# A two-layer backbone step: modulation by channel halves, and table work and scan steps in other places

## What is computed

```
for l in range(2):
    for s in (context, latent):            # with c_ctx and with c
        shift, scale, gate = split(silu(cond[s]) @ w_ada[l] + b_ada[l], 3)
        h = rmsnorm(x[s], norm_g[l]) * (1 + scale) + shift
        z = h @ w_in[l]                    # ca, cg | ssm, sg | q, kv, ag | 3 x 1024 merge
        ya = silu(layernorm(depthwise_conv31(ca * sigmoid(cg))))
        br_a = (ya * silu(conv_gate)) @ w_conv_out[l]
        y  = d * ssm + scan forwards + scan backwards   # complex diagonal state space
        br_b = (glu(gelu(y) @ w_ssm_glu[l]) * silu(sg)) @ w_ssm_out[l]
        q, k = rmsnorm per head (latent: rotary too); latent also reads context keys and values
        br_c = (attention(q, k, v) * silu(ag)) @ w_attn_out[l]
        mixed = sigmoid(m_a) * br_a + sigmoid(m_b) * br_b + sigmoid(m_c) * br_c
        x[s] += gate * (mixed @ w_out[l])
outputs: x of both streams, keys and values of the context, its final scan states
```

## Time and profile before

| | |
|---|---|
| median of 3 runs | 786.66 us (784.63 to 787.0) |
| profiled execution | 783.96 us, its span 782.2 us, mean granted TensorE clock 0.937 |
| TensorE, its weight load | busy 667.8 us (85%), 477.0 us (61%) |
| VectorE, ScalarE, POOL | 567.1 us (73%), 298.8 us (38%), 36.2 us (5%) |
| transfers | 117.65 MB, 46.7% of 16 engines on SP's queue |
| chain that ended last | PE 36%, DVE 13%, ACT 2%, issue 2%, of the span |

### The profile page before, as it was taken

How to read it: one execution, slowest core, us unless ns; L and a number is a source line. 1 busy time by engine, 2 the same in 40 slices (tenths; PEclk the granted TensorE clock), 3 DMA queues, 4 the chain that set the end, 5 groups by cost and what they waited for, 6 DMA issues and landing times.

```text
span 782.2 us, 9620 instructions
## 1 busy us (share of the span) xinstructions
PE 667.8 (85%) x3578; PEld 477.0 (61%) x3578; DVE 567.1 (73%) x1063; ACT 298.8 (38%) x452; POOL 36.2 (5%) x50
## 2 busy tenths in 40 slices
PE   4539999999778799775989499999978679999997
PEld 1337774446644588664768387555556348877875
DVE  3776486794885899889765634948878688998564
ACT  1354351113544244351543534311345334444442
POOL 2010200210000000010000200011000000000000
PEclk9978999999897999986999799999999789999999
DMA  8754267841453556521445145583051025665531
GB/s 252 290 200 134 72 231 252 281 158 33 184 193 113 147 184 181 168 81 32 158 135 160 54 135 197 173 299 109 18 199 28 27 81 162 189 188 161 189 116 54
DMA packets 63209, 117.65 MB, mean 150 GB/s; under 512 B 11052, under 2 KB 15484, under 8 KB 63164
## 3 DMA queue, kind: packets, MB, share of 16 engines
q1 hardware_dynamic: 62988, 116.98, 46.7%
q10 hardware_dynamic: 176, 0.07, 0.0%
HBM read 112.51 MB, written 1.38 MB: 146 GB/s over the span
## 4 chain that ended last, share of the span: by engine, by line
PE 36%; DVE 13%; ACT 2%; issue 2%; POOL 1%; POOLq 0%; DVEq 0%; ACTq 0%
PE proj L1050 8%; PE proj L1052 8%; PE proj L1051 8%; PE proj L767 7%; DVE qkt L1372 3%; DVE H L1372 2%; PE side L782 1%; PE side L990 1%; PE side L899 1%; DVE cvacc L1444 1%; DVE pre L1372 1%; PE side L1068 1%; DVE raw_split L1372 1%; POOL st L1853 1%; DVE mixed L1372 1%
## 5 line engine op out<-in xcount | busy, mean ns | idle before, releaser
L767 PE MATMUL proj<-raw,hT 128*128 128x512 f32 (+1 forms) x320 | 132.0, 558 | 0.0
L1444 DVE SCALAR_TENSOR_TENSOR cvacc<-cvpad,taps,cvacc 128x256 f32<-128x256 f32 x240 | 98.3, 478 | 0.2
L767 PEld LDWEIGHTS proj<-raw,hT 128*128 128x128 f32 x320 | 58.2, 190 | 59.4 <-issue 57.8
L1051 PE MATMUL proj<-raw_split,H_split 128*128 128x512 f32 x224 | 90.1, 402 | 0.0
L1108 ACT ACTIVATE wide_split<-raw 128x1024 fp32r<-128x1024 f32 x59 | 61.9, 1058 | 72.6 <-PE proj L1052 72.6
L1372 DVE TENSOR_TENSOR raw_split<-raw,wide_split 128x1024 fp32r<-128x1024 f32 x59 | 71.4, 1220 | 19.0 <-ACT wide_split L1108 18.5
L1050 PE MATMUL proj<-wide_split,H_split 128*128 128x512 f32 x140 | 58.4, 417 | 15.2 <-DVE raw_split L1372 14.8
L1052 PE MATMUL proj<-wide_split,H_split 128*128 128x512 f32 x140 | 56.5, 403 | 0.0
L1051 PEld LDWEIGHTS proj<-raw_split,H_split 128*128 128x128 f32 x224 | 44.1, 197 | 9.3
L1108 ACT ACTIVATE utok_split<-raw 128x1024 fp32r<-128x1024 f32 x29 | 30.7, 1057 | 37.1 <-PE proj L1052 37.1
L1372 DVE TENSOR_TENSOR raw_split<-raw,utok_split 128x1024 fp32r<-128x1024 f32 x29 | 35.4, 1221 | 10.7 <-ACT utok_split L1108 10.3
(11 more groups left out here) (236 smaller groups left out, 1314.5 us busy)
## 6 DMA issues: line engine op xcount, KB each, us to landing
raw<-in_w_in SPq DMA_DIRECT2D x104, 512.0 KB, 3.7
raw<-in_w_ada SPq DMA_DIRECT2D x48, 512.0 KB, 5.3
raw<-in_w_out SPq DMA_DIRECT2D x16, 512.0 KB, 3.8
raw<-in_w_ssm_glu SPq DMA_DIRECT2D x8, 512.0 KB, 6.8
raw<-in_w_ssm_out SPq DMA_DIRECT2D x8, 512.0 KB, 3.7
raw<-in_w_attn_out SPq DMA_DIRECT2D x8, 512.0 KB, 3.7
raw<-in_w_conv_out SPq DMA_DIRECT2D x8, 512.0 KB, 3.8
raw<-in_w_in SPq DMA_DIRECT2D x8, 256.0 KB, 3.7
```

The costliest lines, as they stand in the source:

```text
L767: m = T.matmul(proj.bank((l, u, s))[:, 0:n], lhs[:, s, kt, :], w[:, i, :], start=(kt == 0), stop=last)
L1051: T.matmul(bank[:, :], hi, wlo, start=False, stop=False)
L1444: m = V.scalar_tensor_tensor(acc, src, taps[:, t, j:j + 1], acc, ALU.mult, ALU.add)
```

## The change

- A modulation slab now holds shift and scale of half the channels (two runs of 512 columns) instead of one of the two for all. `hT` and `early` go by channel half instead of by stream, ScalarE modulates stream 0 and VectorE stream 1. Units cg and ssm run in halves (`HALVED`): two slabs of cg and two of ssm on the first channel half, then the rest.
- In the prologue the loads of x and of the modulation rows stand before those of the table c. The first channel half is normed, split and half of pre made before the rest of the modulation arrives.
- `preP` is taken apart into `bbar` and `pre(l, half)`. In layer 1 too, the second half of pre now stands in unit cg/ssm and its `preE` behind `pack`, ahead of POOL's `bz`. For layer 1's tables, `tabA` moves ahead of C0, `tabB` ahead of C1's `cback`, `bT` and `bbar` behind A0, the first half of pre behind A1 and its `preE` behind the output projection; their loads are issued in comb B0 instead of B1.
- All 32 scan steps stand before attention, six of them ahead of unit q. QK norm squares and sums both streams first, then scales. Twelve convolution taps follow the scan, the first attention has four in each of five parts, the second six, and B0, B1 and C0 have 14, 14 and 10.
- The end of the first attention (a reciprocal and two products) and the gate gg are done within `Y`.

```diff
-    return ([("hT", 0), ("hT", 1), ("early", 0), ("early", 1), ("chunks", "cg"), ("unit", "cg")]
-            + ([("preP", 0, 1)] if l == 0 else [])
-            + [("unit", "ssm"), ("unit", "ca"), ("pack",)] + ([("preE", 0, 1)] if l == 0 else [])
-            + [("bz", 0), ("UT",), ("S",), ("cp",), ("convT", 0), ("convT", 1), ("unit", "q"), ("unit", "kv"),
-               ("adaE", l, 2), ("qkn", 0), ("qkn", 1), ("scan",), ("unit", "sg"), ("K", 0), ("bz", 1),
+    return (([("hT", 0), ("early", 0)] if l else [])
+            + [("chunks", "cg"), ("hT", 1), ("early", 1), ("half", "cg"), ("half", "ssm"), ("unit", "cg"), ("pre", l, 1),
+             ("unit", "ssm"), ("unit", "ca"), ("pack",), ("preE", l, 1),
+             ("bz", 0), ("UT",), ("S",), ("cp",), ("convT", 0), ("convT", 1), ("scan", 0, 6), ("unit", "q"), ("unit", "kv"),
+             ("adaE", l, 2), ("qkn",), ("scan", 6, NCHUNK), ("conv", 12, None), ("unit", "sg"), ("K", 0), ("bz", 1),
...
-            + [("qkT", 0), ("att", 0), ("unit", "gg"), ("Y",), ("adaT", l, 2)] + nxt("adaT", n, 0)
+            + [("qkT", 0), ("att", 0), ("Y",), ("adaT", l, 2)] + nxt("adaT", n, 0)
...
-            + [("chunks", "meB0"), ("brT", "B", 0), ("brT", "B", 1), ("conv", 20, "B0"), ("comb", "B", 0),
-               ("brT", "C", 0), ("brT", "C", 1), ("conv", 20, "B1"), ("comb", "B", 1)]
-            + nxt("small", n) + nxt("cT", n) + [("conv", 20, "C0"), ("comb", "C", 0)]
-            + nxt("taps", n) + nxt("tabA", n) + [("cback", 0), ("cback", 1), ("comb", "C", 1)]
-            + nxt("tabB", n) + nxt("bT", n) + nxt("preP", n, 0) + [("brT", "A", 0), ("brT", "A", 1), ("comb", "A", 0)]
-            + nxt("preE", n, 0) + nxt("preP", n, 1) + [("comb", "A", 1)] + nxt("preE", n, 1)
-            + [("wout", 0), ("wout", 1)] + nxt("xn", n, 0) + nxt("xn", n, 1))
+            + [("chunks", "meB0"), ("brT", "B", 0), ("brT", "B", 1), ("conv", 14, "B0"), ("comb", "B", 0)]
+            + nxt("small", n) + [("brT", "C", 0), ("brT", "C", 1), ("conv", 14, "B1"), ("comb", "B", 1)]
+            + nxt("cT", n) + nxt("tabA", n) + [("conv", 10, "C0"), ("comb", "C", 0)]
+            + nxt("taps", n) + nxt("tabB", n) + [("cback", 0), ("cback", 1), ("comb", "C", 1)]
+            + [("brT", "A", 0), ("brT", "A", 1), ("comb", "A", 0)]
+            + nxt("bT", n) + nxt("bbar", n) + [("comb", "A", 1)] + nxt("pre", n, 0)
+            + [("wout", 0), ("wout", 1)] + nxt("preE", n, 0) + nxt("xn", n, 0) + nxt("xn", n, 1))
...
-                src = A["w_ada"][key[1]].rearrange("(k p) n -> p k n", p=P)
-                slabs.append((key, 1, D, src[:, key[3]:key[3] + 1, D * key[2]:D * key[2] + D]))
+                src = A["w_ada"][key[1]].rearrange("(k p) (r x) -> p k r x", p=P, x=W)[:, key[3], :, :]
+                slabs.append((key, 2, W, src[:, 4:6, :] if key[2] == 2 else src[:, key[2]:4:2, :]))
...
                 elif k == "qkn":
-                    s = stg[1]
...
+                    needs("h")
+                    for s in range(NS):
+                        proj.drained(dve, (l, "q", s))
+                        proj.drained(dve, (l, "kv", s))
+                        link(tt_(qkt[:, :], qk[:, s, :], qk[:, s, :]))
+                        V.tensor_reduce(qst[:, s, 0, :], qkt[:, :].rearrange("p (h d) -> p h d", d=HD), AX_X,
+                                        ALU.add).then_inc(qk_sq, 1)
+                        dve.wait_ge(qk_sq, ls(l, s))
+                    for s in range(NS):
+                        qk_norm(l, s)
...
-                        if s == 0:
-                            c0 = STEPS_BEFORE_ATT + STEPS_IN_ATT * p
-                            for c in range(c0, c0 + STEPS_IN_ATT):
-                                for i in range(4):
-                                    scan_step(l, c, i)
-                        else:
-                            for _ in range(8):
-                                conv_tap(*taps_left.pop(0))
+                        for _ in range(6 if s else 4):
+                            conv_tap(*taps_left.pop(0))
```

More of the change, by code:

```diff
@@ L126, in units_of @@
 def units_of(stage):
-    if stage[0] == "unit":
+    if stage[0] in ("unit", "half"):
         u = stage[1]
@@ L400, in build @@
         slab_used = sem("slab_used")
[L402 to L403 removed]
+        pieces = [key for key in order_of_slabs if key[0] != "ada" and split_unit(key[1])]
         piece_at = {key: m for m, key in enumerate(pieces)}
@@ L1016, in _ @@
                     m.then_inc(side.full, 1)
-                if k in ("unit", "comb", "wout") and stg[1] not in IN_ATT_UNITS:
+                if k in ("unit", "half", "comb", "wout") and stg[1] not in IN_ATT_UNITS:
                     for u, nk, n in units_of(stg):
@@ L1094, in merged_high, with gate @@
                                  ACT.Copy, scale=0.5).then_inc(split_hi, 1)
+            def gate(l, u):
+                for s in range(NS):
+                    key = (l, u, s)
+                    proj.filled(act, key)
+                    S.activation(gates[:, GATE[u], s, :], proj.bank(key)[:, :], ACT.Silu).then_inc(proj.freed(key), 1)
             highs = [0]
@@ L1615, in _ @@
-                        for i in range(2):
-                            side.drained(dve, ("bT", ll, i))
-                        for r in range(2):
-                            t1, t2 = (parts[j][:, :, r if j == 0 else 1 - r, :].rearrange("p c g -> p g c") for j in range(2))
-                            makes("bbar", tt_(bbar[:, r, :, :], t1, t2, ALU.add if r else ALU.subtract))
                         side.filled(dve, ("cT", ll, 1))
-                        needs("bbar")
                     else:
```

256 lines of the change are left out of this document (140 added, 116 removed).

## The result

| | before | changed |
|---|---|---|
| median of 20 runs each, side by side | 784.57 us (782.79 to 787.22) | 787.05 us (785.53 to 788.55) |
| ratio, 95% interval | | 1.0025 (1.0016 to 1.0035) |
| span of the profiled execution | 782.2 us | 784.7 us |
| mean granted TensorE clock | 0.937 | 0.942 |

The change makes the kernel 2.5 us slower: the side that was forecast, at 0.6 of the 4.2 us. The sum was wrong by 1.7 us, and by much more within, since the errors of its terms partly cancel. The forecast of 790.9 stands 3.9 above the measured 787.05; 2.1 of that is its starting point, 786.66, the median of three runs, where the median of twenty is 784.57.

The account below looks back on a forecast made before the run. TensorE's pace was taken as the bound, with gaps nearly all ended by VectorE instructions. Terms 9.0 + 3.2 - 4.7 - 8.1 + 5.0 - 1.1 + 0.9 = +4.2 on the median 786.66 gave 790.9 us, range 780 to 798.

Parts of the forecast that it names:

- term 1: Start of attention: key copy 7.35 us later; +9.0 in layer 1 with a restart, +3.2 in layer 0 with half a one.
- term 2: Scan's output and second attention: earlier HY copy and fewer taps ahead of the GELU sums, -4.7 us over both layers.
- term 6: Prologue: half the modulation needed, but split and half of pre queue on VectorE; +0.9 us (bounds -2 and +2).
- term 3: Layer 0's combinations and output projection: C0 +5.9, C1 -0.95, A0 -17.9, A1 -0.7, output projection +5.55; together -8.1 us.
- Term 4: Layer 1's first projections: pre's other half between two slab residues, with half a restart and 16 transposes, +5.0 us.
- Term 5: From layer 0 to 1: second stream's normalisation without POOL's work beside it, -1.1 us (bounds -2.5 and +1).
- That row is the nearest, so I take 1.5: QK norm: VectorE holds POOL up, as at 705.60, so the rearranged norm saves 1.5 us; ends 0 and 3.65.
- restart: TensorE's clock at 1.2 GHz after a wait: 1.65 us behind longer waits, half (0.8) behind waits near 2.4 us.
- Within the first attention ... so nothing: First attention: four taps (1.65 us) replace two scan steps (2.1), but VectorE waits for TensorE each step; no gain.
- POOL is not held up: Rival, QK norm: saves 3.65 us instead of 1.5, key copy 5.2 later; 785.8 us, chance 0.22.
- The second: Rival: TensorE keeps 2.4 GHz across the new waits, all restarts (6.55 us) fall out; 784.35 us, chance 0.15.
- The third: Rival: the rearranged QK norm saves nothing because POOL's operations are held, +3.8 us; 794.7 us, chance 0.13.

Follow-up runs that it names:

- x_qkn: Changed kernel with the QK norm done one stream after the other, as before; ratio to the kernel before 1.0083, span 789.0 us.
- x_warm: Changed kernel with the key transpose of layer 1's first attention done 48 times instead of once; ratio to the kernel before 0.9995, span 782.7 us.
- x_taps: Changed kernel with the twelve convolution taps ahead of attention put back into the combinations, both layers; ratio to the kernel before 0.994, span 778.9 us.
- x_attend: Changed kernel with the first attention's end done ahead of the scan's output again; ratio to the kernel before 1.0035, span 783.4 us.
- x_att8: Changed kernel with eight taps instead of six per part of the second attention, ten fewer in the combinations; ratio to the kernel before 1.0059, span 788.0 us.
- x_pre0: Changed kernel with layer 1's first half of pre made in the output projection's second half; ratio to the kernel before 0.9947, span 778.9 us.
- x_best3: x_best2 with both halves of layer 0's pre moved behind first units and cut by residues; median 749.99 us, ratio to the kernel before 0.9557.
- x_best2: Changed kernel with x_pre0's move, x_taps in layer 1 alone, and tabA, tabB and pre's second half cut by residues; median 756.42 us, ratio to the kernel before 0.9646.

## Why the prediction was right or wrong, point by point

**The step that failed.** Measured less forecast, the sum was off by -2.3 us in term 1, -2.2 in term 2 and -0.8 in term 6, and by +2.9 in term 3 and +0.5 in terms 4 and 5 together; that +2.5 came out, on the side of the forecast, is these errors cancelling, and so in good part luck. The step that failed is in term 1: "That row is the nearest, so I take 1.5." The QK norm saved 2.54 us in each layer instead, and x_qkn shows 2.6 and 2.7 of it at the key copies, so the term was 1.0 too dear twice. Three smaller steps failed beside it. A restart had one price, 1.65, by the length of the wait; the runs show from 1.4 to 3.0, and none behind the waits of 1.51 and 2.56 to which half a one was given. Term 2 put the shorter filling at nothing and the taps at 1.2 a layer; 0.8 is left for the one, and the other measured 1.45 to 1.6. Term 3 put B0 at nothing; it lost 1.1.

**What bounds the kernel: right in the main.** The waits that the edits moved end with a VectorE instruction: those that the earlier trace rows names, and beside them H_split (403.21) and, in the prologue, pre (53.32). The edits that took VectorE's work from ahead of them gave the time back. Not all long waits are VectorE's, though: in the second attention four of 2.6 to 3.3 us end with ScalarE in the trace of before, and the change hardly moved them.

**Term 1, attention's start: right in layer 1 by two errors, wrong in layer 0.** Layer 1 measured +6.0 for the key copy and +2.9 for the restart (x_warm), 8.9 for a forecast of 9.0. The QK norm saved 2.54 and not 1.5, the twelve taps cost 4.6 and not 4.9 (x_taps), the restart cost 2.9 and not 1.65. The step "That row is the nearest, so I take 1.5" failed: POOL was held up once, by 0.6, and the second time by 0.4, not until the first stream was scaled. The Trainium skill ("SBUF — State Buffer", "Who interferes with whom") has a VectorE instruction with two SBUF inputs contend with a POOL instruction that reads SBUF. The trace agrees in kind, as the 0.84 at 517.27 shows; the size is the measured one, 0.6 and 0.4, and VectorE's own products beside POOL's second root (521.15, two in 1.02) take what they take in x_qkn with POOL idle. In layer 0 the same 6.0, less 4.93, gives 1.0; TensorE then waited 1.51, and "half a restart" did not come. Forecast +3.2, measured +1.0.

**Term 2, scan's output and second attention: direction right, size short.** Measured -4.6 in layer 0 and, with the restart taken out, -2.3 in layer 1, against -2.9 and -1.8. The step "Within the first attention ... so nothing" failed in part: the filling in its last part counts (0.8), and the move of the attention's end counts 1.6 up to the HY copy, though it comes back behind it (x_attend). The taps fewer are worth 1.45 to 1.6 a layer (x_att8), not 1.2. A restart that the term did not have also plays in: behind the 4.04 us at 203.99 the clock of before was 0.50, behind the 2.08 at 202.83 it was 1.00. The other traces of this order, where it fell there, take 0.3 to 0.6 longer in the stretches behind.

**Term 3, combinations: the mechanism right in each stage, the sum 2.9 too good.** A0 (-18.1 for -17.9), A1 and the output projection (+5.6 for +5.55) came as priced, C1 and C0 0.5 and 1.0 worse. C0's wait was 4.76 for 4.25, and the restart behind it 2.5 for 1.65 (twelve slow matmul spacings, 0.43 against 0.23); in C1 it was 2.2 where before it was 1.4 (eleven for seven). B0 and B1 had no price and lost 1.7: 1.1 of it in B0, whose wait is the same (3.31 for 3.26), but whose clock stayed at 0.50 over the first 5.28 us, while the trace of before has

```profile
264.82:270.10 5.28, 5.28 (x17) 4.26 (x18) 4.90 (x8) 0.86 (x1) 0.00 (x0) 0.73 0.41 121
```

In layer 1, B0 of before had the slow stretch too. In layer 0 all eleven traces of the changed order have it, at 0.50 or 0.51 over the first 5 us; whether the 0.73 of before was its rule or chance stays open, since there is one trace of it.

**Term 4, layer 1's units:** +5.4 for +5.0, by two errors. The wait of 2.56 and the transposes of 1.9 are as priced; the half restart behind the wait did not come here (it did in x_pre0), but the one at the first matmul of cg, which had no price, took 2.8 where before it took 1.9. **Term 5:** -1.0 for -1.1. **Term 6:** the first matmul came 1.8 later, not 0.9, and the units took 1.7 less, so +0.1 up to Uz. The 1.7 is what the restart behind 79.70 had cost; behind the same wait at 86.97 none came in this trace, but it came in five of the eight traces of this order. Uz lies between 99.4 and 101.8 in the eight, and at 100.74 before, so this term is nothing within 1.3. "I see no way to get there earlier" was true of the change and false of the kernel: x_best3 starts 11.9 earlier.

**The rivals.** The first ("POOL is not held up") has about half of its price in it: waits of 2.24, not 1.2 or 3.3. The second fell for the long waits: behind 4.76, 6.10, 7.27 and 7.28 the first matmuls take 0.76 to 1.19. Its two half restarts, behind 1.51 and 2.56, did stay away. The third fell with x_qkn.

Together: 8.9 + 1.0 - 6.9 - 5.2 + 5.4 - 1.0 + 0.1 = 2.3, which is, within rounding, the 2.5 of the two spans.

## What to carry to other kernels

A block of work on an engine that only serves another costs what it sticks out beyond the ready buffers at the place where it stands, not its length: the same 8 us of tabA cost 6.9 in one piece and nothing within 0.3 when three slab residues stood between its parts and the ten taps behind it had gone to the stages before (x_best2 did both at once; no run tells them apart). So before moving a block to another stage, cut it where it stands, or look for a stage in which the serving engine waits for the served one (the output projection's 7.5 us), and price a move by the shortest of the covers it passes. A ledger of stretches between the same instructions of two traces tells such prices apart where the total, here 0.25%, hides terms of +9 and -18.

## What the runs showed of the hardware that I had not expected

- A restart of TensorE's clock has no one price. Behind waits of 3.3 us (B0) it cost 1.4 us in one trace and 2.5 in another (seven and twelve slow matmul spacings, 0.43 against 0.23). Behind the wait of 7.3 us for layer 1's key copy it cost 2.1 to 3.0 in five traces with the same code there, and 1.6 behind the 9.96 of x_qkn. The wait of 2.56 us in layer 0's second unit brought one in five executions and none in three, with the same code.
- 48 useless transposes in such a wait (5.90 us of it) kept the clock at 1.00 and gave 2.94 us back, 0.3% of the kernel.
- A VectorE operation with two operands held POOL up for no longer than was left of it: 0.84 against 0.21 us for one POOL operation, which ended with it, and 2.39 against 1.97 for a longer one. VectorE was not held up by POOL there.
